# Two row tiles for scores and gates, and a new order of a body, in a hybrid attention and recurrence layer

## The reference

```python
h = rmsnorm(x, ln_gain)
z = h @ w_in      # q 16x64 | k 4x64 | v 4x64 | g_attn 1024 | x_lru 1024 | g_lru 1024
# head group A: window 128, 16 query heads on 4 key/value heads of 64, a learned sink per head
scores = einsum('bnqhgd,bnkhd->bnhgqk', qb, kc) * HEAD_DIM ** -0.5   # 128 queries x 256 keys
p = exp(scores - m); denom = sum(p) + exp(sink - m)
o = einsum('bnhgqk,bnkhd->bnqhgd', p / denom, vc)
y_attn = rmsnorm(o * silu(g_attn), attn_out_gain)
# head group B: causal conv of width 4, then 16 blocks of 64 channels
u = causal_depthwise_conv(x_lru, conv_w, conv_b)
r = sigmoid(einsum('bsnc,ncd->bsnd', ub, w_r) + b_r)      # 64x64 per block
i = sigmoid(einsum('bsnc,ncd->bsnd', ub, w_i) + b_i)
a = exp(-8 * r * softplus(-lam)); scan h = a * h + sqrt(1 - a**2) * (i * u)
y_lru = rmsnorm(h * silu(g_lru), lru_out_gain)
out = rmsnorm(x + concat([y_attn, y_lru]) @ w_out, final_gain)
```

## Time and profile before

| what | value |
|---|---|
| median of 3 runs | 1423.26 us (1422.8 to 1424.64) |
| the profiled execution's own time | 1424.16 us |
| its span, first to last instruction | 1422.6 us |
| PE busy | 1377.9 us (97%), 6464 matmuls |
| PEld busy | 1134.5 us (80%) |
| DVE busy | 1008.3 us (71%) |
| ACT busy | 765.3 us (54%) |
| POOL busy | 314.1 us (22%) |
| mean granted TensorE clock | 0.997 |

### The profile page before, as it was taken

One profiled execution on the slowest core, in us unless ns is written; L12 is line 12 of the kernel. 1 busy time (PEld: TensorE's weight loads), 2 busy tenths in 40 slices (PEclk: granted clock), 3 DMA queues, 4 the chain that ended last, 5 costly groups with the idle time before them and its releaser, 6 DMA issues.

```text
span 1422.6 us, 21721 instructions
## 1 busy us (share of the span) xinstructions
PE 1377.9 (97%) x6464; PEld 1134.5 (80%) x6464; DVE 1008.3 (71%) x1725; ACT 765.3 (54%) x1551; POOL 314.1 (22%) x316
## 2 busy tenths in 40 slices
PE   5999999999999999999999999999999999999998
PEld 4778777888888887888888888788877888888886
DVE  4798989987777878787787877787886644344442
ACT  5677686756566574757566574657565322222120
POOL 2131413232231414232231413232230000000000
PEclk9999999999999999999999999999999999999999
DMA  8767676763636364554636374554717333232320
GB/s 218 252 241 245 244 236 234 258 199 146 225 119 222 140 215 150 186 185 146 222 128 230 127 276 144 186 173 170 224 50 248 118 89 116 61 118 86 91 89 30
DMA packets 151872, 243.27 MB, mean 171 GB/s; under 512 B 35456, under 2 KB 101248, under 8 KB 151808
## 3 DMA queue, kind: packets, MB, share of 16 engines
q1 hardware_dynamic: 144784, 217.86, 45.6%
q0 software_dynamic: 7024, 24.65, 5.2%
HBM read 179.55 MB, written 62.91 MB: 170 GB/s over the span
## 4 chain that ended last, share of the span: by engine, by line
PE 45%; DVE 21%; issue 18%; ACT 9%; POOL 3%; SPq 1%; DMA 1%; DVEq 1%; ACTq 1%; POOLq 0%
PE ring L1414 20%; PE acc_b L201 12%; PE ring L201 11%; DVE hs L1287 5%; POOL ri L622 2%; DVE p_lo L1224 2%; ACT p_sb L838 2%; DVE s_sb L1198 2%; PE ps_v L1464 2%; DVE cu L1253 1%; DVE smax L1211 1%; DVE o_sb L1233 1%; ACT cu L862 1%; ACT kc_ol L851 1%; DVE ya L1184 1%
## 5 line engine op out<-in xcount | busy, mean ns | idle before, releaser
L1414 PE MATMUL ring<-split,w_hi 128*128 128x512 f32 x2304 | 719.1, 393 | 7.8 <-DVE split L1026 7.2
L1414 PEld LDWEIGHTS ring<-split,w_hi 128*128 128x128 f32 x2304 | 427.1, 189 | 94.9 <-DVE split L1026 8.0
L1414 PE MATMUL ring<-split,w_lo 128*128 128x512 f32 x1152 | 450.4, 391 | 0.0
L1414 PEld LDWEIGHTS ring<-split,w_lo 128*128 128x128 f32 x1152 | 216.8, 188 | 46.6
L838 ACT ACTIVATE p_sb<-s_sb,smax 128x129 f32<-128x129 f32 x256 | 99.9, 393 | 118.7 <-DVE smax L1211 118.5
L622 POOL TENSOR_TENSOR ri<-ri,hs 128x512 f32<-128x512 f32 x32 | 53.9, 1704 | 383.0 <-ACT hs L904 383.0
L1253 DVE SCALAR_TENSOR_TENSOR cu<-xl,prm,cu 128x512 f32<-128x512 f32 x96 | 72.2, 752 | 43.0 <-ACT cu L862 34.0
L778 ACT ACTIVATE q_st<-qrot 64x512 fp32r<-64x512 f32 x64 | 40.4, 631 | 114.9 <-DVE qrot L1089 114.1
L201 PE MATMUL acc_b<-wo_rest,y_own 128*128 128x512 f32 x384 | 89.9, 390 | 2.9 <-DVE wo_rest L162 2.3
L201 PE MATMUL ring<-split,y_own 128*128 128x512 f32 x384 | 91.3, 392 | 0.1
L1685 ACT ACTIVATE w_hi<-res 128x1024 fp32r<-128x1024 f32 x15 | 15.9, 1060 | 134.3 <-DVE res L1755 134.3
(11 more groups left out here) (203 smaller groups left out, 2478.0 us busy)
## 6 DMA issues: line engine op xcount, KB each, us to landing
w_hi<-w_split_scratch SPq DMA_DIRECT2D x108, 512.0 KB, 3.2
w_lo<-w_split_scratch SPq DMA_DIRECT2D x108, 512.0 KB, 4.3
w_split_scratch<-w_hi SPq DMA_DIRECT2D x36, 512.0 KB, 5.1
w_split_scratch<-w_lo SPq DMA_DIRECT2D x36, 512.0 KB, 5.7
w_raw<-w_in_d SPq DMA_DIRECT2D x32, 512.0 KB, 4.4
y_scratch<-hs POOLq DMA_DIRECT2D x32, 256.0 KB, 5.4
y_scratch<-ya POOLq DMA_DIRECT2D x16, 512.0 KB, 8.7
rows<-y_scratch SPq DMA_DIRECT2D x8, 1024.0 KB, 7.0
```

Source lines behind the costliest of these rows:

```text
L1414: last = mm(bank(r), w[:, i % WSLOTS, k, :], h[:, par, k, :], start=(k == 0 and j == 0), stop=(k == KC - 1 and j == 2))
```

## The change

The new order on PE is: XL0, XL1, `score(0)`, `gates(0)`, GL0, `gates(1)`, `score(1)`, GA0, `turn_p(0)`, `score(2)`, GA1, `weigh_v(0)`, `turn_p(1)`, `score(3)`, `turn_x`, GL1, `weigh_v(1)`, `turn_p(2)`, KVG, `weigh_v(2)`, `turn_p(3)`, Q0, `weigh_v(3)`, Q1, `turn_v`. The lists of the other engines follow it, the ring's order and the order of the weight loads too. `softmax_a` is cut into `select` and `top`, `gather_o` into `add_o` and `gate_o`, `lru_mid` into `one_less` and `input_x`, `decays` into `take_r`, `take_i` and `decays`.

Scores and gates use the array as two row tiles of 64 rows, tile 0 on partitions 0 to 63 and tile 1 on 64 to 127. The queries' high and low parts stand in two tensors `q_hi` and `q_lo` with two heads on the two halves of the partitions, and a head takes three matmuls of 64 rows. The gate weights are dense 64x64 blocks side by side: the first half holds r|i in its columns, the second i|r, and each half's results go to a bank of its own, so that the two banks hold r and i crosswise.

```diff
-XL0, GL0, XL1, GA0, GA1, GL1, KVG, Q0, Q1 = range(9)
+XL0, XL1, GL0, GA0, GA1, GL1, KVG, Q0, Q1 = range(9)
-(R_XL0, R_GL0, R_XL1, R_R0, R_I0, R_GA0, R_R1, R_I1, R_GA1, R_XT0, R_XT1, R_GL1, R_KV, R_Q0, R_Q1,
+(R_XL0, R_XL1, R_R0, R_I0, R_GL0, R_R1, R_I1, R_GA0, R_GA1, R_XT0, R_XT1, R_GL1, R_KV, R_Q0, R_Q1,
...
-        gw_hi = sb("gw_hi", [P, UNITS, 2, P], F32R)
+        gw_hi = sb("gw_hi", [P, UNITS, P], F32R)
...
                 load(XL0, COL_XL)
-                load(GL0, COL_GL)
+                load(XL1, COL_XL + P)
...
-                        sp.dma_start(gw_raw[rows, :, j, rows],
+                        at = (j + half) % 2
+                        sp.dma_start(gw_raw[rows, :, at * BW:(at + 1) * BW],
...
+                load(GL0, COL_GL)
...
             def high_q(n, j):
...
-                for half in range(2):
-                    rows = slice(half * HD, (half + 1) * HD)
-                    nc.scalar.activation(q_st[rows, 2 * j + half, :], qrot[rows, :], ACT.Copy
-                                         ).then_inc(*q_high.one())
+                nc.scalar.activation(q_hi[:, j, :], qrot[:, :], ACT.Copy).then_inc(*q_high.one())
...
+                def take_r(u):
...
+                    for to, r in ((lower, R_R[u]), (upper, R_I[u])):
+                        nc.scalar.activation(ra[u][to, :], bank(r)[to, :], ACT.Tanh, scale=0.5,
+                                             bias=prm[to, G, C_BR:C_BR + 1]).then_inc(*gate_r.one())
...
+                def take_i(u):
...
+                    for to, r, rows in ((lower, R_R[u], upper), (upper, R_I[u], lower)):
+                        nc.scalar.activation(ri[u][to, :], bank(r)[rows, :], ACT.Tanh, scale=0.5,
+                                             bias=prm[to, G, C_BI:C_BI + 1]).then_inc(*ring_act.one())
...
             def low_q(n, j):
...
+                dve.wait_ge(*q_high.at(n, j + 1))
+                nc.vector.tensor_tensor(q_lo[:, j, :], qrot[:, :], f(q_hi[:, j, :]), ALU.subtract
+                                        ).then_inc(*q_low.one())
...
                 if not last:
+                    low_k(n, following)
                     turn_q(n, 0)
...
+                add_o(3)
+                gate_o(3)
...
+                    add_q(n, 0)
+                    low_q(n, 0)
+                    previous_v(n, following)
+                    turn_q(n, 1)
+                    differ_v(n)
+                    low_v(n, following)
...
                     add_q(n, 1)
                     low_q(n, 1)
-                    low_v(n, following)
...
-                    for h in range(GQ):
-                        for k, st, sp_ in ((k_hi, True, False), (k_lo, False, True)):
-                            last = mm(ps_s[:, h, :], q_st[:, h, b * BLK:(b + 1) * BLK],
-                                      k[:, b * BLK:(b + 2) * BLK], start=st, stop=sp_)
+                    for j in range(2):
+                        for i, (v, k) in enumerate(((q_hi, k_hi), (q_hi, k_lo), (q_lo, k_hi))):
+                            for half in range(2):
+                                rows = slice(half * HD, (half + 1) * HD)
+                                last = mm(ps_s[:, 2 * half + j, :], v[rows, j, b * BLK:(b + 1) * BLK],
+                                          k[rows, b * BLK:(b + 2) * BLK], start=(i == 0), stop=(i == 2))
...
-                        for i, (w, v) in enumerate(((gw_hi, u_hi), (gw_hi, u_lo), (gw_lo, u_hi))):
-                            last = mm(bank(r), w[:, u, j, :], v[:, :], start=(i == 0), stop=(i == 2))
-                        last.then_inc(*ring_ready.one())
+                    for i, (w, v) in enumerate(((gw_hi, u_hi), (gw_hi, u_lo), (gw_lo, u_hi))):
+                        for half in range(2):
+                            rows = slice(half * BW, (half + 1) * BW)
+                            ins = mm(bank((R_R, R_I)[half][u]), w[rows, u, :], v[rows, :], start=(i == 0), stop=(i == 2))
+                            if i == 2:
+                                ins.then_inc(*ring_ready.one())
...
                 project(n, XL0, par, split)
-                project(n, GL0, par, split)
                 project(n, XL1, par, split)
                 score(0)
                 gates(0)
-                project(n, GA0, par, split)
+                project(n, GL0, par, split)
                 gates(1)
                 score(1)
-                project(n, GA1, par, split)
+                project(n, GA0, par, split)
                 turn_p(0)
                 score(2)
+                project(n, GA1, par, split)
+                weigh_v(0)
+                turn_p(1)
+                score(3)
                 if q < NQUART - 1:
                     turn_x()
                 project(n, GL1, par, split, q < NQUART - 1)
-                weigh_v(0)
-                turn_p(1)
-                score(3)
+                weigh_v(1)
+                turn_p(2)
```

More of the change, by code:

```diff
@@ L666, in body @@
                     sine_q(n, 0)
-                p_current(n, 3)
-                if not last:
                     sine_q(n, 1)
@@ L1535, in body @@
                         proj.chunk(pe, ring, 1, e)
-                weigh_v(3)
-                if not last:
-                    turn_v(n)
             iterations(pe, body)
```

277 lines of the change are left out of this document (141 added, 136 removed).

## The result

| kernel | median | ratio to before, 95% interval |
|---|---|---|
| before | 1423.95 us | |
| changed | 1412.93 us (1411.73 to 1413.11) | 0.992 [0.9902, 0.9937] |

The account below looks back on a forecast made before the run. PE's own list was taken to bound the kernel. From 1424.16 us, less 15.4 for scores, 22.4 for gates and 21 for the order, plus 28 for switches, gave 1393 us; range 1370 to 1448.

Parts of the forecast that it names:

- Tiles and loads overlap: Scores and gates: both row tiles' matmuls and weight loads run side by side, saving 15.4 us and 22.4 us in all.
- rivals 2 and 3: Scores and gates: loads go one at a time, 1433 us, chance 0.26; or nothing overlaps, 1461 us, chance 0.08.
- A switch at 0.22 us: Eight changes of tiling a body on PE, 128 in all, cost 0.22 us each, 28 us in all.
- rival 5: A change of tiling on PE is nearly free, 0.05 us, giving 1372 us; chance 0.12.
- The net of the array: PE's array work: what the tiles give, 37.8 us, less the switching, leaves a gain of 9.6 us.
- A steady body of 61.9 us: Later bodies, 63.7 us before, fall to 61.9 us by tiles, switches and removed waits.
- The waits of the earlier trace: `weigh_v(0)` waiting for POOL and `weigh_v(3)` for DVE: the new order removes both, 1.2 us a steady body.
- 1.2 us to spare, and I count nothing: Before `gates(0)`: u_lo comes at 11.1 us after Q1's end, PE asks at 12.3, so no wait is counted.
- ACT's four more reads are hidden: Tanh of r and i by halves adds 2.8 us on ACT, net 1.2 a body, hidden behind PE.
- I count only 7 us for the whole quarter: First quarter's four bodies: the new order gains 7 us, of 9.1 us they lie above steady ones.
- rival 4: `gates(0)` waits for u as late as before, 2.3 us in 16 bodies, giving 1430 us; chance 0.10.
- little in the last: Last quarter: the order gains 1.2 us in three bodies and little in the last, 4.5 us in all.

Follow-up runs that it names:

- order_only: The new order with the old 128-row scores and gates and q in halves, no row tiles, against the changed kernel; 1436.1 us, 1.0071 of before.
- tiles_only: The order of the kernel before, with scores and gates in two row tiles and ACT's reads by halves as in the changed kernel; 1474.8 us, 1.0339 of before.
- gates_tiled: The changed kernel's new order with only the gates in row tiles; scores of 128 rows and q in halves; 1435.1 us, 1.0067 of before.
- split_pool: The changed kernel with the first quarter's three splits of the next body's weights done by POOL instead of DVE; 1426.3 us, 1.0013 of before.

## Why the prediction was right or wrong

**Tiles and loads overlap: right.** 3 to 5 ns between the halves, 0.12 and 0.23 us between pairs; rivals 2 and 3 fall. The Trainium skill's page TensorE: Matmul & The Clock Gate, Packing small matmuls, says that matmuls of different row groups start about 4 ns apart and that loads overlap with matmuls in flight in other row groups; the 3 to 5 ns here agree. Its section LDWEIGHTS says that a load's time goes by its columns and not by its rows, and the trace agrees (0.19 us for a load of 64x128 as for one of 128x128). The queue of loads, which the prediction held possible, did not come.

**A switch at 0.22 us: right in size,** 0.2 measured; rival 5 falls. The Trainium skill's page TensorEngine Tiling (Array Packing), Key Properties, says that a change of tiling mode drains TensorE; the trace fits that, since the 0.16 us that the tail alone would cost is a little under what was measured, but it doesn't show a drain by itself. The net of the array was forecast as 0.6 us a body (9.6 in 16) and is 0.8 by the table of waits.

**A steady body of 61.9 us: right within 0.3.** The waits of the earlier trace rows went as said (1.2 forecast, 1.1 to 1.2 in order_only). But the step "1.2 us to spare, and I count nothing" was off by about 1.6 us. The chain from XL0's end takes 5.7 to 6.7 us and not 5.2, and u is late by 0 to 0.6 us in the changed kernel's steady bodies (0.4 in the ninth). It would be by 1.5 without the whole `high_q` and `low_q`, an effect that the prediction priced as busy time of ACT and DVE only and not as a shorter chain.

**ACT's four more reads are hidden: right in the steady bodies, not shown elsewhere.** With tiles_only they delay u: the cover was not ACT's idle time but their place on its list. In the first quarter both kernels with these reads wait for o_sb, 4.3 and 5.0 us, and the two without don't.

**The first quarter, "I count only 7 us for the whole quarter": this is the step that failed.** The forecast had the quarter 9.4 us shorter, the 7 and a quarter of the array's 9.6, and it is 16.5 longer: 25.9 us off, which is more than the whole miss of 20. The order's own term is measured by order_only, 18.2 us more where 7 less was counted; no row was given for the 7. The wrong path behind it is the chain for u, which was followed from a steady body, and used for all 16. In the first quarter DVE has three splits of 1.21 us on the same stretch, and the chain measured 10.3 us from XL0's end, against 5.2 in the forecast (11.1 less 5.9) and 6.4 of cover. By starts, the four bodies lie 33 us above the 61.8 that a body takes without waits: 15.5 before `gates(0)`, 8.0 by the lower clock behind it, and 7.7 at the waits for o_sb and for a split. The prediction did name this: rival 4 with "DVE has 60 of 65.6 us in the first quarter" for it. Its mechanism is what happened, in 4 of 16 bodies. It gave 2.3 us a body; the wait is 3.3 to 3.9, and the lower clock behind it adds 2.0 at its place, which the prediction didn't have at all. The number was there: the kernel before has u_lo 10.4 us behind XL0's end in its third body, and 6.4 of cover leaves 4.0 of wait. So it should have been a term of the sum and not a rival.

**The end, "little in the last" body: too small, and it hid part of the miss.** The last three bodies before the last one, the last body and phase B are 14.2 us shorter where 6.9 were forecast (4.5 by the order, 2.4 in the array). Up to phase B's first one-column matmul the last body takes 68.2 us before, 65.1 in order_only and 63.4 in the changed kernel: the waits there for p_lo and w_lo are gone, 2.4 us. Of the 2.1 us behind that point 1.8 are waits of PE for DVE (2.9 us before, 1.1 now). With this the forecast's other terms came 6 us better than counted; without that luck the time would have been 1419.

**The chances.** Rival 4 was priced as all bodies or none. A mechanism tied to a load that only one quarter has should have been split by quarter: 4 x (3.7 + 2.0) is 23 us, which with the 7 us gain taken back gives 1423. The measured 1413 lies 10 below: 6 from the other terms, and 4 that the quarter did better than this sum.

## What to carry to other kernels

Follow the chain that a reorder shortens the cover of in each kind of body, above all in the one where the helping engine is fullest, and not in the steady one alone. A projection taken away between a producer and its user is a loan from the slack of every engine on the chain: here 5.6 us of cover went, the steady bodies had it to within 0.6 us, and the first quarter did not. When one wait is removed in a stretch where the engines behind PE have little slack, expect it back one step later: five runs shortened or covered the way to u, and none took more than 10.7 us out of the quarter, which had grown by 16.5. And before work is given to an engine that looks idle, look in the trace for what its neighbour's operations take beside it.

## What the runs showed of the hardware

- The two row tiles' matmuls and weight loads start 3 to 5 ns apart, and the price of changing between 128 rows and two tiles of 64 is 0.2 us each way, half of it on the first matmul and half on the second.
- Behind the waits of 3.3 to 3.9 us before `gates(0)` the granted clock was at its lower level, 0.51 in the window from 199 to 203 us. Behind waits of 0.3 to 1.5 us in the steady bodies of order_only and gates_tiled it wasn't, but in tiles_only it fell, behind waits of PE of which none in that body was longer than 1.7 us:

```profile
490.60:494.00 3.40, 3.40 (x13) 2.82 (x11) 2.58 (x3) 3.39 (x13) 1.97 (x3) 0.50 0.13 53
```

- A multiply `ya<-ya,o_sb` of DVE, 128x256, takes from 0.41 to 2.2 us in the same body; the long ones lie beside work of POOL. The mean is 0.96 in the first quarter and 0.94 behind it, so it doesn't explain the difference between the two. With a weight split on POOL beside it, it takes 4.68 us, an add of 128x512 2.87 for 0.68, and a subtraction of 128x256 2.58 for 0.41 (split_pool).
